# Four weight units of the first feed-forward panel have their low parts subtracted on GpSimd

## The chip, the cores and the metric

The kernel runs on one core of one Trainium2 chip. The metric is the device time of one execution in microseconds (us). Before the change it is 1159.51 us, the median of 3 runs (1159.35 to 1160.35).

Names: PE is TensorE, DVE is VectorE, ACT is ScalarE, POOL is GpSimd, SP is SyncE, which issues the loads.

## The reference

One decoder layer on 256 tokens of width 2048, all in float32. What matters here is the middle: an output projection with a residual, an RMS norm, and the feed-forward part of width 5632.

```python
h = h + jnp.concatenate([o_attn, o_conv], axis=-1) @ w_out[i]
f = rmsnorm(h, g_ffn[i])
h = h + (jax.nn.silu(f @ w_gate[i]) * (f @ w_up[i])) @ w_down[i]
```

## The kernel before, in words

**Every matrix product is done in parts.** A float32 operand is split into a high part (`hi`, rounded to the matmul's input type by a copy) and a low part (`lo`, the raw value minus `hi`). A product is then three matmuls: hi by hi, hi by lo and lo by hi. The weights stream from memory, so each piece of weights is split on the chip before its matmuls.

**The weights move in units.** Unit m is 128 partitions by 1024 numbers, half of a raw slot of 1 MB. Three steps handle it: ACT writes `w_hi` (line 666), then DVE or POOL writes `w_lo` (`split_lo`, line 993 on DVE and line 590 on POOL), then PE runs the unit's 12 matmuls. The units are numbered through the program. Unit 80 begins the output projection (`WO_A`), units 112 to 127 (`FFN0` to `LOOP0` - 1) are the first panel of 512 columns of the feed-forward part, and from 128 (`LOOP0`) on come ten passes of the main loop, the last panel and the gates.

**Slots.** `w_hi` and `w_lo` have four slots each, unit m uses slot m % 4. So ACT may write unit m + 4 only when PE has finished unit m (`slot_free`), and it does so about three units ahead of PE's need.

**Who subtracts.** `by_pool(m)` decides. Before the change POOL takes every fourth unit from 8 on and every second one from 40 up to 95; from unit 96 on DVE subtracts all. PE waits for the unit on the semaphore of the engine that subtracts it (`arrived`), and SP waits for both before it loads new weights over the raw slot (`slot_split`).

**The order is written out by hand.** Each engine has its own program, and its instructions run strictly one after the other. DVE and ACT go through steps m; step m ends with the split of unit m + 4. Around the change DVE's steps hold more than splits, because the main loop's products need the normed activations in another form:

- line 1277 in step 117: a row of scales is copied to `rb`
- line 1223 (`normalise`), two in each of the steps 118 to 121, tiles of 128x512 in `w_sum`
- lines 1238 to 1243 (`x_sums`), four sums of 128x256, in steps 119 and 120
- line 1229 (`a_lo`) in steps 119 to 123 and 125, and line 1249 (`s_lo`) in steps 120 and 121: low parts of what these gave; ACT makes their high parts (lines 873 and 878), the one of line 878 just ahead of units 124 and 125
- step 127: `first_swiglu` (line 1209), which waits for PE to finish the first panel; the main loop's first steps come right behind it on DVE.

All of these except line 1277 and line 1209 are two-input operations with both inputs in SBUF.

**POOL's program** after unit 95: eight additions that join the high and low parts of the activations (`join_x`, line 596), with a tiny `pow` (line 584) between the sixth and the seventh, then another tiny `pow` (`root(2, 3)`) that waits until the gates near the end of the kernel. Between 359.6 and 1072 us POOL does nothing.

Of the kernel before, what the change touches and what calls it, by code (L numbers as in the profile page):

```python
# [67 lines left out]
FFN0 = WO_C + 16  # L68
LOOP0 = FFN0 + 16
# [30 lines left out]
OUT_VECTOR = [(0, slice(0, 2 * NP)), (1, slice(0, NP)), (1, slice(NP, 2 * NP))]  # L100
OUT_SCALAR = [(0, slice(2 * NP, 3 * NP)), (1, slice(2 * NP, 11 * NP // 4)), (1, slice(11 * NP // 4, 7 * D // 8))]
POOL_HALF, POOL_UNTIL = 40, WO_C

# [27 lines left out]


def by_pool(m):
    return 8 <= m < POOL_UNTIL and (m % 4 == 3 or m % 2 == 1 and m >= POOL_HALF)


def lo_count(m, it=0):

    return sum(by_pool(i) == by_pool(m) for i in range(m + 1)) + PER_LOOP * it
# [32 lines left out]
def hybrid_decoder_layer(nc, x, p, g_mix, w_in, w_dw, b_dw, g_conv_ln, b_conv_ln, w_out, g_ffn,  # L174
# [11 lines left out]
    with ExitStack() as ctx:  # L186
# [85 lines left out]
        def x_norm(i):  # L272

            return w_sum[:, i].rearrange("p (k t) -> p k t", k=2)
# [93 lines left out]
        def slot_free(engine, m, it=0):  # L368

            if LAST <= m < LAST + 4:  # L370
                engine.wait_ge(half_done, PG0)
            elif m >= LAST + 4:
                engine.wait_ge(half_done, m - 2 * SLOTS + 1)
            elif LOOP0 + SLOTS <= m < LOOP0 + LOOP_SLOTS:

                engine.wait_ge(half_done, FFN0)
            elif in_loop(m) and m >= LOOP0 + LOOP_SLOTS:
                engine.wait_ge(half_done, m - slot_back(m) + 1 + PER_LOOP * it)
            elif PLE0 <= m < PLE0 + SLOTS:
                engine.wait_ge(half_done, m - PER_LOOP % LOOP_SLOTS + 1)  # L380
            elif m >= SLOTS:
                engine.wait_ge(half_done, m - SLOTS + 1)
# [49 lines left out]
        def _(sp):  # L432
            def slot_split(n, it=0):

                if n >= RAW:
                    last = 2 * (n - RAW) + 1
                    if by_pool(last):
                        sp.wait_ge(lo_ready, lo_count(last - 1))
                        sp.wait_ge(lo_ready_pool, lo_count(last))
                    else:  # L440
                        sp.wait_ge(lo_ready, lo_count(last, it))
# [125 lines left out]
        def _(pool):  # L567
# [11 lines left out]
            def root(norm, order, tiles=slice(0, TT)):  # L579

                if order == 0:
                    pool.wait_ge(consts_ready, 2)
                pool.wait_ge(msq_ready, order + 1)
                nc.gpsimd.tensor_tensor(rstd[:, norm, tiles], msq[:, norm, tiles], power[:, tiles], ALU.pow).then_inc(rstd_ready, 1)  # L584

            def split_lo(m):
                pool.wait_ge(hi_ready, m + 1)
                slot_free(pool, m)
                rows = slice(2 * (m % 2), 2 * (m % 2) + 2)
                nc.gpsimd.tensor_tensor(w_lo[:, m % SLOTS], w_raw[:, (m // 2) % RAW, rows],  # L590
                                        w_hi[:, m % SLOTS].bitcast(F32), ALU.subtract).then_inc(lo_ready_pool, 1)

            def join_x(i):

                pool.wait_ge(nT_ready, 4 + i // 2 + 1)
                nc.gpsimd.tensor_tensor(x_norm(i), nT_hi[:, 2 * i:2 * i + 2].bitcast(F32), nT_lo[:, 2 * i:2 * i + 2].bitcast(F32),
                                        ALU.add).then_inc(x_joined, 1)

            for m in filter(by_pool, range(POOL_UNTIL)):
                if m == AHEAD + 15:  # L600
                    root(0, 0)
                if m == AHEAD + 51:

                    pool.wait_ge(conv_step, CONV_OPS)
                    nc.gpsimd.tensor_tensor(group_sum[:, :, :], conv[:, 0:2], conv[:, 2:4], ALU.add).then_inc(conv_added, 1)
                    pool.wait_ge(conv_added, 1)
                    nc.gpsimd.tensor_tensor(group_sum[:, 0], group_sum[:, 0], group_sum[:, 1], ALU.add).then_inc(conv_added, 1)
                if m == AHEAD + MEAN_AT - 2:

                    pool.wait_ge(conv_step, 2 * CONV_OPS)  # L610
                    nc.gpsimd.tensor_tensor(u[:, 4:6, 0:T], conv[:, 4:6], conv[:, 6:8], ALU.add).then_inc(conv_added, 1)
                    pool.wait_ge(conv_added, 3)
                    nc.gpsimd.tensor_tensor(group_sum[:, 1], u[:, 4, 0:T], u[:, 5, 0:T], ALU.add).then_inc(conv_added, 1)
                if m == AHEAD + MEAN_AT + 2:
                    root(4, 1)
                if m == AHEAD + MEAN_AT:

                    for i in range(2):
                        pool.wait_ge(dev_squared, 2 * i + 2)
                        nc.gpsimd.tensor_tensor(u[:, 4 * i:4 * i + 2, 0:T], u[:, 4 * i:4 * i + 2, 0:T],  # L620
                                                u[:, 4 * i + 2:4 * i + 4, 0:T], ALU.add).then_inc(dev_added, 1)
                    pool.wait_ge(dev_added, 2)
                    nc.gpsimd.tensor_tensor(u[:, 0:2, 0:T], u[:, 0:2, 0:T], u[:, 4:6, 0:T], ALU.add).then_inc(dev_added, 1)
                split_lo(m)
# [2 lines left out]
            root(1, 2)  # L627
            for i in range(6, QUADS):
                join_x(i)
            root(2, 3)  # L630
            pool.wait_ge(rows_loaded, 32)
            for c in range(3):
# [1252 lines left out]
```

## Time and profile before

| | |
|---|---|
| median of 3 runs | 1159.51 us |
| the profiled execution | 1159.4 us |
| its span, first to last instruction | 1157.6 us |
| PE busy | 1142.3 us |
| DVE busy | 936.4 us |
| ACT busy | 717.0 us |
| POOL busy | 125.1 us |
| granted TensorE clock, mean | 0.998 |

The span is what the profile shows; 1.8 us of the profiled time lie around it. A busy PE means that matmuls follow each other without a gap, so each gap on PE is time that the kernel could be shorter, unless something else then comes in its place. The rows below have the first panel's units 121 to 127 between 369 and 389 us.

### The profile page before, as it was taken

To read this page: it belongs to the slowest core of one execution; us is meant where nothing else is said; L and a number is where in the kernel's file an instruction comes from. 1 tells how busy PE (TensorE), PEld (TensorE's weight loads), DVE (VectorE), ACT (ScalarE), POOL (GpSimd) and SP (SyncE) were. 2 spreads that over 40 slices of the span, in tenths; PEclk is the share of its full clock that TensorE was granted. 3 is DMA by queue.
4 is the path that set the end of the run, shared out by engine and by line. 5 is a ranking of instruction groups with operands and counts; after the bars stand their busy time and mean duration, and the time that the engine had idled before them with its cause. 6 is when DMAs were issued, how large, how long until landed. Compare 5 with 4: busy or idle time off the path is not lost.

```text
span 1157.6 us, 16551 instructions
## 1 busy us (share of the span) xinstructions
PE 1142.3 (99%) x5591; PEld 963.7 (83%) x5591; DVE 936.4 (81%) x1244; ACT 717.0 (62%) x990; POOL 125.1 (11%) x74
## 2 busy tenths in 40 slices
PE   9999999999999899999999999999999999999996
PEld 8889989988888678888888888888888888888886
DVE  6589767768677897989888898989798988847674
ACT  6544465456555576676767667676667676767552
POOL 0222443435031000000000000000000000000111
PEclk9999999999999999999999999999999999999999
DMA  9655554554555466575646564655647565484541
GB/s 343 217 182 182 182 181 158 172 170 158 189 175 181 146 227 209 170 241 171 234 165 226 176 247 149 227 180 193 232 160 242 178 228 172 153 317 152 202 158 73
DMA packets 113120, 223.38 MB, mean 193 GB/s; under 512 B 5193, under 2 KB 6417, under 8 KB 112816
## 3 DMA queue, kind: packets, MB, share of 16 engines
q1 hardware_dynamic: 112608, 222.08, 56.8%
q8 instruction: 29, 0.48, 0.2%
q10 hardware_dynamic: 464, 0.66, 0.2%
q14 instruction: 19, 0.16, 0.0%
HBM read 220.63 MB, written 2.10 MB: 192 GB/s over the span
## 4 chain that ended last, share of the span: by engine, by line
PE 91%; DVE 4%; issue 2%; ACT 1%; POOL 1%; DVEq 0%; POOLq 0%; ACTq 0%
PE ps L1679 11%; PE ps L1681 11%; PE ps L1680 11%; PE ps L1478 8%; PE ps L1476 8%; PE ps L1477 8%; PE ps L1463 6%; PE ps L1464 6%; PE ps L1465 6%; PE ps L1510 3%; PE ps L1509 3%; PE ps L1508 3%; PE ps L1518 2%; DVE w_lo L993 1%; PE ps L1672 1%
## 5 line engine op out<-in xcount | busy, mean ns | idle before, releaser
L666 ACT ACTIVATE w_hi<-w_raw 128x1024 fp32r<-128x1024 f32 (+1 forms) x308 | 304.2, 996 | 205.2 <-PE ps L1478 120.2
L993 DVE TENSOR_TENSOR w_lo<-w_raw,w_hi 128x1024 fp32r<-128x1024 f32 (+1 forms) x272 | 317.0, 1175 | 135.4 <-ACT w_hi L666 135.1
L1476 PE MATMUL ps<-w_hi,nT_hi 128*128 128x512 f32 x280 | 111.4, 398 | 0.0
L1478 PE MATMUL ps<-w_hi,nT_lo 128*128 128x512 f32 x280 | 109.1, 390 | 0.0
L1477 PE MATMUL ps<-w_lo,nT_hi 128*128 128x512 f32 x280 | 109.0, 389 | 0.0
L666 ACT ACTIVATE w_hi<-arena 128x1024 fp32r<-128x1024 f32 x58 | 61.6, 1062 | 73.9 <-DVE arena L1268 28.1
L590 POOL TENSOR_TENSOR w_lo<-w_raw,w_hi 128x1024 fp32r<-128x1024 f32 x36 | 86.7, 2408 | 181.9 <-ACT w_hi L666 181.9
L1049 DVE SCALAR_TENSOR_TENSOR ps<-arena,taps,ps 128x256 f32<-128x256 f32 x232 | 94.7, 485 | 0.2 <-ACT ps L787 0.2
L584 POOL TENSOR_TENSOR rstd<-msq,power 128x2 f32<-128x2 f32 x4 | 2.8, 707 | 724.4 <-DVE msq L1024 723.2
L993 DVE TENSOR_TENSOR w_extra<-w_raw,w_extra 128x1024 fp32r<-128x1024 f32 (+1 forms) x70 | 78.7, 1136 | 0.0
L1679 PE MATMUL ps<-w_hi,nT_hi 128*128 128x512 f32 x195 | 76.8, 394 | 0.0
L1681 PE MATMUL ps<-w_hi,nT_lo 128*128 128x512 f32 x195 | 76.0, 390 | 0.0
L1680 PE MATMUL ps<-w_lo,nT_hi 128*128 128x512 f32 x195 | 75.9, 389 | 0.0
L1508 PE MATMUL ps<-nT_hi,w_hi 128*128 128x256 f32 x256 | 72.9, 285 | 0.0
L1510 PE MATMUL ps<-nT_hi,w_lo 128*128 128x256 f32 x256 | 72.4, 283 | 0.0
L1509 PE MATMUL ps<-nT_lo,w_hi 128*128 128x256 f32 x256 | 72.4, 283 | 0.0
L993 DVE TENSOR_TENSOR w_lo<-arena,w_hi 128x1024 fp32r<-128x1024 f32 x58 | 69.1, 1220 | 0.0
L666 ACT ACTIVATE w_extra<-w_raw 128x1024 fp32r<-128x1024 f32 (+1 forms) x70 | 67.6, 980 | 0.5 <-PE ps L1681 0.2
L1476 PE MATMUL ps<-w_hi,oT_hi 128*128 128x512 f32 x160 | 63.5, 397 | 0.0
L853 ACT ACTIVATE ps<-h 128x512 f32<-128x512 f32 x80 | 44.9, 594 | 28.3 <-DVE arena L1271 26.7
L1478 PE MATMUL ps<-w_hi,oT_lo 128*128 128x512 f32 x160 | 62.4, 390 | 0.0
L1477 PE MATMUL ps<-w_lo,oT_hi 128*128 128x512 f32 x160 | 62.3, 389 | 0.0
(271 smaller groups left out, 2809.3 us busy)
## 6 DMA issues: line engine op xcount, KB each, us to landing
w_raw<-in_w_gate SPq DMA_DIRECT2D x88, 512.0 KB, 3.9
w_raw<-in_w_up SPq DMA_DIRECT2D x88, 512.0 KB, 4.8
w_raw<-in_w_down SPq DMA_DIRECT2D x44, 1024.0 KB, 5.1
w_raw<-in_w_in SPq DMA_DIRECT2D x32, 1024.0 KB, 5.1
w_raw<-in_w_out SPq DMA_DIRECT2D x16, 1024.0 KB, 5.0
w_raw<-in_w_pgate SPq DMA_DIRECT2D x16, 1024.0 KB, 5.1
w_raw<-in_w_in SPq DMA_DIRECT2D x14, 512.0 KB, 9.5
w_raw<-in_w_ple SPq DMA_DIRECT2D x2, 1024.0 KB, 5.8
```

The lines of the kernel that those rows point to most:

```text
L666: nc.scalar.activation(tiles_of(m, first)[0], source_of(m, first), ACT.Copy).then_inc(hi_ready, 1)
L993: nc.vector.tensor_tensor(lo, source_of(m, first), hi.bitcast(F32), ALU.subtract).then_inc(lo_ready, 1)
L1049: ins = nc.vector.scalar_tensor_tensor(dst, u[:, c, tap:tap + T], taps[:, c, tap:tap + 1], conv_sum(c), ALU.mult, ALU.add)
L1476: nc.tensor.matmul(banks[t][:, :], x_hi[:, k, rows], hi[:, k], start=start, stop=False)
L1477: nc.tensor.matmul(banks[t][:, :], x_hi[:, k, rows], lo[:, k], start=False, stop=False)
L1478: ins = nc.tensor.matmul(banks[t][:, :], x_lo[:, k, rows], hi[:, k], start=False, stop=stop)
L1508: nc.tensor.matmul(dst, w_hi[:, s, k, cols], x_hi[:, k], start=start, stop=False, skip_group_check=True)
L1509: nc.tensor.matmul(dst, w_hi[:, s, k, cols], x_lo[:, k], start=False, stop=False, skip_group_check=True)
L1510: ins = nc.tensor.matmul(dst, w_lo[:, s, k, cols], x_hi[:, k], start=False, stop=stop, skip_group_check=True)
L1679: nc.tensor.matmul(bank[:, :], x[0], w[0], start=first, stop=False)
L1680: nc.tensor.matmul(bank[:, :], x[0], w[1], start=False, stop=False)
L1681: return nc.tensor.matmul(bank[:, :], x[1], w[0], start=False, stop=last)
```

## The change

POOL takes the low parts of units 121, 123, 125 and 127. `by_pool` names them, so `arrived`, `slot_split` and the counts of both semaphores follow, DVE's program leaves them out, and POOL's program gets four calls of its `split_lo` between the last `join_x` and `root(2, 3)`.

```diff
 POOL_HALF, POOL_UNTIL = 40, WO_C
+POOL_FFN = range(FFN0 + 9, LOOP0, 2)
...
 def by_pool(m):
-    return 8 <= m < POOL_UNTIL and (m % 4 == 3 or m % 2 == 1 and m >= POOL_HALF)
+    return m in POOL_FFN or 8 <= m < POOL_UNTIL and (m % 4 == 3 or m % 2 == 1 and m >= POOL_HALF)
...
             for i in range(6, QUADS):
                 join_x(i)
+            for m in POOL_FFN:
+                split_lo(m)
             root(2, 3)
```

The three added lines move the lines behind them by one to three: line 993 is 996 in the changed kernel, line 590 is 591, line 1223 is 1226, 1229 is 1232, 1249 is 1252.

DVE's program before, from the end of step 120 on. The first and the last `w_lo` here are the splits of units 124 and 128; the rows with `arena,rb` are `normalise`, those with `nT_lo` are `a_lo`, and the one with `oT_lo` is `s_lo`:

```order
236 L993 TENSOR_TENSOR w_lo<-w_raw,w_hi 128x1024
237 L1223 TENSOR_TENSOR arena<-arena,rb 128x512 x2
238 L1229 TENSOR_TENSOR nT_lo<-arena,nT_hi 128x512
239 L1249 TENSOR_TENSOR oT_lo<-arena,oT_hi 128x1024
240 L993 TENSOR_TENSOR w_lo<-w_raw,w_hi 128x1024
241 L1229 TENSOR_TENSOR nT_lo<-arena,nT_hi 128x512
242 L993 TENSOR_TENSOR w_lo<-w_raw,w_hi 128x1024
243 L1229 TENSOR_TENSOR nT_lo<-arena,nT_hi 128x512
244 L993 TENSOR_TENSOR w_lo<-w_raw,w_hi 128x1024 x2
```

The same place in the changed kernel:

```order
234 L996 TENSOR_TENSOR w_lo<-w_raw,w_hi 128x1024
235 L1226 TENSOR_TENSOR arena<-arena,rb 128x512 x2
236 L1232 TENSOR_TENSOR nT_lo<-arena,nT_hi 128x512
237 L1252 TENSOR_TENSOR oT_lo<-arena,oT_hi 128x1024
238 L1232 TENSOR_TENSOR nT_lo<-arena,nT_hi 128x512
239 L996 TENSOR_TENSOR w_lo<-w_raw,w_hi 128x1024
240 L1232 TENSOR_TENSOR nT_lo<-arena,nT_hi 128x512
241 L996 TENSOR_TENSOR w_lo<-w_raw,w_hi 128x1024
```

The splits of unit 125 (row 240 of before) and of unit 127 (the first of the two in row 244) are gone from DVE; the splits of 124, 126 and 128 stand where they stood.

POOL's program in the changed kernel, from its last split before the feed-forward part on. The last `x4` row of `w_lo` is new; before, the row of `rstd` behind it followed the two additions directly:

```order
27 L591 TENSOR_TENSOR w_lo<-w_raw,w_hi 128x1024 x3
28 L597 TENSOR_TENSOR arena<-nT_hi,nT_lo 128x512 x6
29 L585 TENSOR_TENSOR rstd<-msq,power 128x2
30 L597 TENSOR_TENSOR arena<-nT_hi,nT_lo 128x512 x2
31 L591 TENSOR_TENSOR w_lo<-w_raw,w_hi 128x1024 x4
32 L585 TENSOR_TENSOR rstd<-msq,power 128x2
```

Only these four instructions were added to POOL's queue, and what stands behind them there is not due until the gates.

## Rows read from the trace of the kernel before

**Rows 1.** The page: the span, and each engine's busy time, share and instructions.
```profile
span 1157.6 us, 16551 instructions
PE 1142.3 (99%) x5591; PEld 963.7 (83%) x5591; DVE 936.4 (81%) x1244; ACT 717.0 (62%) x990; POOL 125.1 (11%) x74
```

**Rows 2.** Windows: stretch, length, busy us (instructions) of PE, PEld, DVE, ACT, POOL; clock, DMA, GB/s.
```profile
400.00:410.00 10.00, 7.25 (x30) 5.22 (x30) 9.96 (x12) 6.83 (x9) 0.00 (x0) 1.00 0.64 204
...
1150.00:1157.00 7.00, 0.00 (x0) 0.00 (x0) 2.29 (x7) 1.12 (x2) 0.55 (x1) 0.66 0.42 150
```

**Rows 3.** Timeline of PE, 379 to 406 us: start, duration, operation, [idle before, releaser].
```profile
379.65 0.39 PE L1673 MATMUL ps<-w_lo,nT_hi 128*128 128x512 f32 x1
379.88 0.39 PE L1674 MATMUL ps<-w_hi,nT_lo 128*128 128x512 f32 x1
380.57 0.50 PE L1672 MATMUL ps<-w_hi,nT_hi 128*128 128x512 f32 x1 [0.31 <-DVE w_lo L993]
...
405.78 0.50 PE L1679 MATMUL ps<-w_hi,oT_hi 128*128 128x512 f32 x1 [2.35 <-DVE w_lo L993]
```

**Rows 4.** Timeline of DVE, 362 to 390 us.
```profile
362.41 1.23 DVE L993 TENSOR_TENSOR w_lo<-w_raw,w_hi 128x1024 fp32r<-128x1024 f32 x1 [1.45 <-ACT w_hi L666]
363.56 1.29 DVE L1223 TENSOR_TENSOR arena<-arena,rb 128x512 f32<-128x512 f32 x2
...
367.82 0.42 DVE L1239 TENSOR_TENSOR arena<-arena 128x256 f32<-128x256 f32 x1
...
369.55 1.22 DVE L993 TENSOR_TENSOR w_lo<-w_raw,w_hi 128x1024 fp32r<-128x1024 f32 x1
370.69 1.28 DVE L1223 TENSOR_TENSOR arena<-arena,rb 128x512 f32<-128x512 f32 x2
...
375.22 1.22 DVE L993 TENSOR_TENSOR w_lo<-w_raw,w_hi 128x1024 fp32r<-128x1024 f32 x1
376.35 1.29 DVE L1223 TENSOR_TENSOR arena<-arena,rb 128x512 f32<-128x512 f32 x2
...
379.30 1.22 DVE L993 TENSOR_TENSOR w_lo<-w_raw,w_hi 128x1024 fp32r<-128x1024 f32 x1
...
381.03 1.22 DVE L993 TENSOR_TENSOR w_lo<-w_raw,w_hi 128x1024 fp32r<-128x1024 f32 x1
...
385.64 1.23 DVE L993 TENSOR_TENSOR w_lo<-w_raw,w_hi 128x1024 fp32r<-128x1024 f32 x1
387.50 1.23 DVE L993 TENSOR_TENSOR w_lo<-w_raw,w_hi 128x1024 fp32r<-128x1024 f32 x1 [0.63 <-ACT w_hi L666]
389.95 1.41 DVE L1209 SCALAR_TENSOR_TENSOR arena<-ps,rstd,arena 128x512 f32<-128x512 f32 x2 [1.22 <-ACT arena L840]
```

**Rows 5.** Timeline of ACT, 366 to 379 us: high parts of units 123, 125 and 127.
```profile
366.76 1.06 ACT L666 ACTIVATE w_hi<-w_raw 128x1024 fp32r<-128x1024 f32 x1 [1.14 <-PE ps L1674]
...
374.56 1.05 ACT L666 ACTIVATE w_hi<-w_raw 128x1024 fp32r<-128x1024 f32 x1
...
377.64 1.06 ACT L666 ACTIVATE w_hi<-w_raw 128x1024 fp32r<-128x1024 f32 x1
```

**Rows 6.** Timeline of POOL, 32 to 278 us, three of its operations.
```profile
32.19 2.70 POOL L590 TENSOR_TENSOR w_lo<-w_raw,w_hi 128x1024 fp32r<-128x1024 f32 x1 [29.98 <-ACT w_hi L666]
...
273.10 2.37 POOL L590 TENSOR_TENSOR w_lo<-w_raw,w_hi 128x1024 fp32r<-128x1024 f32 x1
...
277.39 2.39 POOL L590 TENSOR_TENSOR w_lo<-w_raw,w_hi 128x1024 fp32r<-128x1024 f32 x1
```

**Rows 7.** Timeline of DVE beside them.
```profile
32.08 0.56 DVE L1074 TENSOR_TENSOR log_count<-log_count,multiple 128x384 f32<-128x384 f32 x1
...
273.13 3.43 DVE L993 TENSOR_TENSOR w_lo<-w_raw,w_hi 128x1024 fp32r<-128x1024 f32 x1
...
278.29 2.58 DVE L993 TENSOR_TENSOR w_lo<-w_raw,w_hi 128x1024 fp32r<-128x1024 f32 x1 [0.47 <-ACT w_hi L666]
```

**Rows 8.** POOL's line 590, all of it: duration ns min/median/max, first and last start.
```profile
L590 POOL TENSOR_TENSOR w_lo<-w_raw,w_hi x36: 2373/2402/2698, 32.2 to 288.0; 128x1024 fp32r<-128x1024 f32 x36
```

## The prediction, made before the changed kernel ran

> **What bounds the kernel now.** I read the page first: PE is busy for 1142.3 of 1157.6 us [rows 1], so only its gaps can be won, 15.3 us in all. Then PE's waits in order of time. Between the fill at the start and the end of the kernel they stand in one place, the end of the first feed-forward panel and the 35 us behind it, and all of them are for low parts from DVE: the first at 380.57 us, the largest at 405.78 us [rows 3]. The window of 400 to 410 us shows why: PE 7.25 us busy, DVE 9.96 us, POOL 0 [rows 2]. So DVE bounds this stretch, POOL is free, and the change takes work from the one and gives it to the other. Last I read DVE's timeline there [rows 4] and looked for places where DVE and POOL worked side by side [rows 6, 7], since that is what the change brings.
>
> Which row is which unit: the split that starts at 362.41 us is unit 121's, at 369.55 unit 123's, at 375.22 unit 124's, at 379.30 unit 125's, at 381.03 unit 126's, at 385.64 unit 129's, at 387.50 unit 130's [rows 4]. The high parts of 123, 125 and 127 start at 366.76, 374.56 and 377.64 us [rows 5]. PE starts unit 125 at 380.57 [rows 3]. One matmul follows another after 0.227 us (379.65 to 379.88 [rows 3], and eleven more like it), so a unit of 12 takes 2.72 us: unit 124 starts at 377.4, unit 126 at 380.57 + 2.72 + 0.12 = 383.4 us. The 0.12 is the longer first matmul after a gap (0.50 against 0.39 us [rows 3]).
>
> **What can be won.** Of the gaps only the first lies in front of `first_swiglu`. It costs 380.57 - 379.88 - 0.23 = 0.46 us. The later ones come at the end of a DVE chain that starts when PE has finished the panel: DVE sat idle for 0.63 us at 387.50 and 1.22 us at 389.95 us [rows 4], so it had caught up by then, and work taken from it earlier doesn't start that chain sooner than PE does. So the largest gain is 0.46 us, 0.04%. The 4.6 us that DVE no longer spends on four splits (1.14 us each, 369.55 to 370.69 [rows 4]) are not a gain by themselves. Unit 121's falls into idle time at once: DVE was idle for 1.45 us before it [rows 4], and its next split, of 122, waits for ACT as before.
>
> **What a split on POOL costs.** It takes 2.40 us (median of 36 [rows 8]) against 1.14. POOL has time: its program has nothing else that is due before the gates, and a unit's high part is ready two units ahead of PE. The question is what it does to DVE. Three places show it. At 273.10 both start a split; POOL's ends at 275.47, DVE's takes 3.43 us and ends at 276.56, which is 1.09 us after POOL's end. At 277.39 POOL's ends at 279.78 and DVE's at 280.87, again 1.09 us later [rows 6, 7]. So DVE did its whole 1.1 us of work behind POOL's. The other way round, POOL's split at 32.19 took 2.70 us in place of 2.40 beside a DVE addition that had begun 0.11 us before. So two operations that each read two tiles of SBUF don't overlap on the two engines: one holds and the other stands still. I take 2.35 us for one hold (start to start less the overlap of two records). Everything that DVE runs between 366 and 387 us is of that kind, and it runs nearly without idle time. There a split moved to POOL saves DVE 1.14 us and stops it for 2.35.
>
> The Trainium skill says the same in *SBUF — State Buffer*, "Who interferes with whom": a VectorE instruction with two SBUF inputs contends with a GpSimd instruction that reads SBUF, and whoever issues first keeps the others out for the whole instruction. It speaks against this change, and by "whoever issues first" a waiting GpSimd gets the next turn even while VectorE has work lined up; no row here shows such a case, and the sum for it follows from rows.
>
> **Step by step, POOL getting its turn at the next end of a DVE operation.**
>
> - Unit 121: POOL from 362.4 to 364.8, DVE has nothing that is due in it but ends the two `normalise` at 362.2. Nothing gained or lost.
> - Unit 123: high part ready at 366.76 + 1.06 = 367.82 [rows 5]. DVE is then in `x_sums` (367.82 [rows 4]); POOL takes over at about 368.2 and DVE resumes at 370.55, 2.4 late. It then skips the split of 123 (1.14): `normalise` of step 120 starts at 371.9 in place of 370.69. DVE is 1.2 us behind. PE needs 123 at 374.7: in time.
> - Unit 124, on DVE: 375.22 + 1.2 = 376.4 to 377.6. PE wants it at 377.4: a first gap of 0.2 to 0.3 us.
> - Unit 125: its high part stands behind that of `s_hi` on ACT, which waits for the second `x_sums`, so it ends at 375.61 + 1.2 = 376.8. POOL starts when DVE's split of 124 ends, 377.55, and ends at 379.9. PE needs it at about 380.5: the old gap of 0.46 is gone, the new one of 0.25 is there.
> - Unit 127: high part ready at about 379 (377.64 + 1.06, and a little later behind unit 123's slot). POOL asks at once after 125 and gets another 2.35 us, either directly or after one DVE operation of 0.6 us. Both lie ahead of unit 126's split on DVE.
> - Unit 126, on DVE: `normalise` of step 121 is late by 1.2 + 2.35 + 2.35 = 5.9 us; the split of 125 in between is gone, so 126 starts at 381.03 + 5.9 - 1.14 = 385.8 and ends at 387.0 us. PE has finished unit 125 at 383.4 and waits 3.7 us. It starts 126 at 387.1 in place of 383.4: **+3.7 us**.
> - Behind it: the split of 127 is gone from DVE too, which leaves it 5.9 - 2.3 = 3.6 us late, the same as PE; 128 to 130 are in time again. Unit 127's end and `first_swiglu` move by 3.7 us, and the chain behind them, with the gaps up to 422 us, moves as a whole. ACT and SP: the raw slot of units 126 and 127 is freed some 3 us later, no more than PE is late, and its next weights are unit 138's, ten units on, so the load hides.
>
> Sum: 3.7 us on the profiled 1159.4 gives 1163.1, and with the median 0.1 above the profiled execution **1163.2 us**, 0.3% slower. In short: three holds (7.05) less two splits (2.3) less the 1.15 us by which DVE was early for unit 126, and 0.1 for the restart.
>
> **Rivals.**
>
> - *POOL must wait until DVE's queue runs dry.* DVE's operations begin before the last has quite ended (1.14 us apart at 1.22 us each), and POOL may never get in between. It gets in for 123 at a small dependence gap of `x_sums`, but for 125 there is none from 377.5 to the end of `a_lo(5)`, which is the start of 129's split: 385.64 - 376.35 = 9.3 us of run [rows 4] less two splits gives 377.5 + 7.0 = 384.5. POOL ends at 386.9, and PE starts unit 125 there in place of 380.57: +6.3, **1165.8 us**. For it: nothing in the trace excludes it, since every shared stretch before has DVE idle behind one operation. Against it: in [rows 6, 7] POOL got in 0.3 us after it asked. With an idle stretch of 6.7 us on PE the clock could fall as well: it fell to half after PE's last matmul, in a stretch that shows a mean of 0.66, while 2.35 us of idle left it at 1.00 [rows 2]. Each 12-matmul unit at half clock would add 2.7 us, so up to 1168.5.
> - *The holds don't hurt here.* If DVE's operations of 0.3 to 0.7 us slipped in between, or if the stretches of [rows 7] had another cause, POOL's splits would be free: DVE would be 1.14 to 3.4 us ahead, the gap at 380.57 goes, and the time is 1159.5 - 0.46 = **1159.0 us**, not slower. It decides as long as all holds together cost DVE less than the two splits it saves before unit 126, 2.3 us, plus its 1.15 us of lead. For it speaks that POOL has 2 units of time for each split; against it the two equal 1.09 us.
> - *Part of it*: one of the three holds falls into a time when DVE waits for ACT, or 127's comes after unit 126. Then 7.05 becomes 4.7: +1.3 us, 1160.8, and unless 127 is then itself late, it stays there.
>
> **Numbers.** POOL in turn 55%, POOL starved 25%, part of it 8%, no cost 12%. The likeliest gives 1163.2. The range of 8 in 10 leaves out no cost and the part of the starved case in which the clock falls: 1160.8 to 1167.0 us. What a measurement of this kernel can tell from no change is about 0.2%, 2.3 us. The first two cases are slower by more; part of it and no cost lie within 0.2%, but for a little of the former and of the turn's own spread to either side; a gain over 0.2% would need more than DVE's gaps before 389 us hold: 1%. So faster 0.01, same 0.18, slower 0.81.
>
> **What would show it.** In the changed kernel's profile: four POOL splits between 362 and 390 us; DVE's `x_sums` or `normalise` operations of over 2 us beside them, ended at POOL's end plus their own length; a PE gap of 3 to 4 us before unit 126, waiting for DVE (right), or of 6 us before unit 125, waiting for POOL (starved); gaps at 399 to 422 us of the same length as before, only later. Wrong, if DVE's operations keep 0.69 and 1.22 us while POOL runs, if PE has no gap over 1 us before `first_swiglu`, or if the gaps behind it shrink.

## The result, and the profile after

The changed kernel takes 1165.26 us, the median of 6 runs (1163.44 to 1165.50), against 1159.51 before. Over all runs that are compared the ratio is 1.0042, with an interval of 1.0032 to 1.0052. That is 4.9 us slower, between 3.7 and 6.0. (The two medians are 5.7 us apart, since four of the six executions of the kernel before that ran beside it took 1159.35 to 1159.51 us, which by the later ones is its rarer, quicker kind; see unit 123 below.)

The profiled execution took 1165.5 us. Of the 6.1 us that were added to the span of [rows 1], 3.3 are PE's busy time, although it runs the same 5591 matmuls: some of them were slower. The other 2.8 are gaps.

```profile
span 1163.7 us, 16555 instructions
PE 1145.6 (98%) x5591; PEld 966.3 (83%) x5591; DVE 939.1 (81%) x1240; ACT 717.6 (62%) x990; POOL 135.9 (12%) x78
```

DVE's busy time went up by 2.7 us although four splits left it. The reason stands in POOL's timeline and in DVE's beside it, 362 to 395 us (start, duration, operation; line 1226 is `normalise`, 1244 is in `x_sums`):

```profile
362.47 2.40 POOL L591 TENSOR_TENSOR w_lo<-w_raw,w_hi 128x1024 fp32r<-128x1024 f32 x1 [2.92 <-ACT w_hi L669]
367.91 2.59 POOL L591 TENSOR_TENSOR w_lo<-w_raw,w_hi 128x1024 fp32r<-128x1024 f32 x1 [3.04 <-ACT w_hi L669]
376.76 5.82 POOL L591 TENSOR_TENSOR w_lo<-w_raw,w_hi 128x1024 fp32r<-128x1024 f32 x2 [6.26 <-ACT w_hi L669]
```

```profile
365.14 1.23 DVE L996 TENSOR_TENSOR w_lo<-w_raw,w_hi 128x1024 fp32r<-128x1024 f32 x1 [2.78 <-ACT w_hi L669]
...
368.16 2.62 DVE L1244 TENSOR_TENSOR arena<-arena 128x256 f32<-128x256 f32 x1
...
371.76 1.29 DVE L1226 TENSOR_TENSOR arena<-arena,rb 128x512 f32<-128x512 f32 x2
...
376.29 1.22 DVE L996 TENSOR_TENSOR w_lo<-w_raw,w_hi 128x1024 fp32r<-128x1024 f32 x1
377.42 5.71 DVE L1226 TENSOR_TENSOR arena<-arena,rb 128x512 f32<-128x512 f32 x2
...
385.39 1.21 DVE L996 TENSOR_TENSOR w_lo<-w_raw,w_hi 128x1024 fp32r<-128x1024 f32 x1
...
394.91 1.41 DVE L1212 SCALAR_TENSOR_TENSOR arena<-ps,rstd,arena 128x512 f32<-128x512 f32 x2 [1.50 <-ACT arena L843]
```

An operation of 0.42 us took 2.62, and the two `normalise` of step 121 took 5.71 in place of 1.29 [rows 4]. Asked for one by one in that stretch:

```profile
L1226 DVE TENSOR_TENSOR arena<-arena,rb x2: 2892/2892/2893, 377.4 to 380.2; 128x512 f32<-128x512 f32 x2
```

Each was held for 2.21 us (2.89 less 0.68). POOL's two splits and DVE's two operations took turns one by one. The split of unit 126 begins at 385.39; before, it was 381.03 [rows 4].

PE's timeline (the gap stands in brackets). Unit 124 starts at 377.65, 0.25 us after the 377.4 of the kernel before. The first long gap is the one before unit 126; the one at 380.57 [rows 3] is gone, and the last answers to 405.78 of [rows 3]:

```profile
377.65 0.47 PE L1675 MATMUL ps<-w_hi,nT_hi 128*128 128x512 f32 x1
...
382.95 0.39 PE L1677 MATMUL ps<-w_hi,nT_lo 128*128 128x512 f32 x1
386.66 0.50 PE L1675 MATMUL ps<-w_hi,nT_hi 128*128 128x512 f32 x1 [3.32 <-DVE w_lo L996]
...
388.66 0.63 PE L1676 MATMUL ps<-w_lo,nT_hi 128*128 128x512 f32 x1
...
410.74 0.50 PE L1682 MATMUL ps<-w_hi,oT_hi 128*128 128x512 f32 x1 [2.38 <-DVE w_lo L996]
```

And windows of the same kernel (columns as in [rows 2]; the clock is the third number from the right). From 388 to 391 us, right behind the first gap, and from 412 to 415, behind the last, the granted clock is 0.51 and 0.50, which is 1.2 of the 2.4 GHz, and matmuls come 0.43 us apart in place of 0.23:

```profile
388.00:391.00 3.00, 3.00 (x9) 2.32 (x8) 2.08 (x3) 0.00 (x0) 0.00 (x0) 0.51 0.89 332
...
412.00:415.00 3.00, 3.00 (x8) 2.35 (x9) 3.00 (x3) 2.54 (x4) 0.00 (x0) 0.50 0.92 320
```

The tally of the two profiled executions: PE starts unit 126 3.2 us later (386.66 against the 383.4 worked out above). `first_swiglu` is 4.96 us later (394.91 - 389.95), so another 1.7 us was lost in units 126 and 127, at half clock. The span is 6.1 us longer, so the last 1.1 us came behind it, where the second stretch at half clock lies. That last part is not the change's, as the runs below show.

### The profile page after: what moved, and what is told of

Its sections match the earlier page's. It is cut to its first block, busy times and chain, and to the rows that moved or that the text cites. A ratio compares the mean times of both kernels' runs of the same rounds, so it can differ in the third digit from the quotient of the medians.

```text
span 1163.7 us, 16555 instructions
## 1 busy us (share of the span) xinstructions
PE 1145.6 (98%) x5591; PEld 966.3 (83%) x5591; DVE 939.1 (81%) x1240; ACT 717.6 (62%) x990; POOL 135.9 (12%) x78
## 4 chain that ended last, share of the span: by engine, by line
PE 92%; DVE 4%; issue 2%; ACT 1%; POOL 1%; POOLq 0%; DVEq 0%; ACTq 0%
PE ps L1682 11%; PE ps L1683 11%; PE ps L1684 11%; PE ps L1481 8%; PE ps L1479 8%; PE ps L1480 8%; PE ps L1468 6%; PE ps L1467 6%; PE ps L1466 6%; PE ps L1513 3%; PE ps L1511 3%; PE ps L1512 3%; PE ps L1521 2%; PE ps L1675 1%; PE ps L1677 1%
## 5 line engine op out<-in xcount | busy, mean ns | idle before, releaser
L996 DVE TENSOR_TENSOR w_lo<-w_raw,w_hi 128x1024 fp32r<-128x1024 f32 (+1 forms) x268 | 312.2, 1173 | 138.5 <-ACT w_hi L669 137.9
L591 POOL TENSOR_TENSOR w_lo<-w_raw,w_hi 128x1024 fp32r<-128x1024 f32 x40 | 97.5, 2439 | 194.2 <-ACT w_hi L669 194.2
```

The lines of the kernel that those rows point to most:

```text
L996: nc.vector.tensor_tensor(lo, source_of(m, first), hi.bitcast(F32), ALU.subtract).then_inc(lo_ready, 1)
```

## The experiments

Each is compared with runs of the kernel before on the same chip; ratios have their 95% intervals.

**Single units.** The set `POOL_FFN` of the changed kernel is cut down:

```diff
-POOL_FFN = range(FFN0 + 9, LOOP0, 2)
+POOL_FFN = (FFN0 + 9,)                # only_121
+POOL_FFN = (FFN0 + 11,)               # only_123
+POOL_FFN = (FFN0 + 13, FFN0 + 15)     # only_125_127
```

Unit 121:

> POOL takes the split of unit 121 alone. Theory of the holds: POOL runs it at 362.5 to 364.8 us, where DVE has nothing that reads two tiles, so no operation of DVE is stretched, DVE's idle time before the split of 122 grows by 1.1 us, and the time is that of the kernel before: 1159.5 us, within 0.3. Rival (a split on POOL costs wherever it stands, by its 2.4 us or by the extra semaphore): slower by about a quarter of the change's 5.7 us, 1160.9.

Measured: ratio 0.9999 (0.9990 to 1.0008), 1160.26 us beside 1160.17. Its POOL and DVE timelines:

```profile
362.16 2.40 POOL L591 TENSOR_TENSOR w_lo<-w_raw,w_hi 128x1024 fp32r<-128x1024 f32 x1 [2.91 <-ACT w_hi L669]
```

```profile
364.83 1.23 DVE L996 TENSOR_TENSOR w_lo<-w_raw,w_hi 128x1024 fp32r<-128x1024 f32 x1 [2.77 <-ACT w_hi L669]
```

POOL's split ends as DVE, which had been idle for 2.77 us, begins. Nothing is stretched, and the interval leaves no room for the 1.4 us of the rival, so a split on POOL as such costs nothing that this run can see.

Unit 123:

> POOL takes the split of unit 123 alone. Holds: one operation of DVE near 368 us takes about 2.6 us, DVE is 1.2 us late from there, PE's gap before unit 125 grows from 0.5 to 1.7 us and the one before 126 stays away: +1.2 us, 1160.7. Rival (the loss comes only from POOL being late for 125 and 127): no change, 1159.5.

Measured: ratio 1.0006 (0.9997 to 1.0015), 1160.81 beside 1160.17. DVE and PE:

```profile
368.16 2.62 DVE L1244 TENSOR_TENSOR arena<-arena 128x256 f32<-128x256 f32 x1
```

```profile
381.63 0.50 PE L1675 MATMUL ps<-w_hi,nT_hi 128*128 128x512 f32 x1 [0.98 <-DVE w_lo L996]
```

The hold and the later start of unit 125 (381.63 against 380.57 [rows 3], +1.06) are as expected. The median rose by 0.6 us and its interval holds both 0 and the forecast 1.2. The record says why. The executions of a kernel fall into two groups by the mean of the granted clock that each reports. For the kernel before, in all the rounds of these experiments, 17 of 70 executions have 0.998 and took 1159.26 to 1159.71 us, the other 53 have 0.995 to 0.997 and took 1159.93 to 1160.94. Of this kernel 6 of 10 are in the group at 0.998, with 1160.46 to 1160.83, and 4 in the other, with 1161.02 to 1161.65. Group against group the medians differ by 1.1 and 1.2 us, which is the forecast. (The groups were formed after the runs, so this supports the size and is no test of it.)

Units 125 and 127:

> POOL takes 125 and 127 alone. Holds: both fall between the split of 124 and that of 126 on DVE, two operations of DVE take 2.9 us, the split of 126 ends near 385.9 and PE starts 126 2.5 us later than before; with the clock falling after such a gap another 1.5 to 3 us: 1162.0 without the fall, 1163.5 to 1165 with it. Rival (the three holds are not additive, one of them does the harm): the full 1165.

Measured: ratio 1.0023 (1.0014 to 1.0033); the median of 1162.46 beside 1160.17 hides a spread of 1161.84 to 1164.91. DVE and PE:

```profile
376.43 5.73 DVE L1226 TENSOR_TENSOR arena<-arena,rb 128x512 f32<-128x512 f32 x2
```

```profile
385.68 0.50 PE L1675 MATMUL ps<-w_hi,nT_hi 128*128 128x512 f32 x1 [2.62 <-DVE w_lo L996]
```

Two holds, and unit 126 starts 2.3 us later than before (385.68 against 383.4), near the forecast 2.5. The rival's full 1165 is not the median. The profiled execution took 1164.56 us and has the clock at 0.85 from 380 to 390; six of the ten took 1161.84 to 1162.47. So at least the 2.3 us of the wait seem to be in every execution, while the price of the clock comes and goes. Only the one execution was profiled.

**The saving without POOL.** DVE's four splits are shrunk to 8 of each 512 columns. The rest of these low parts is left out.

```diff
+                src = source_of(m, first)
+                if m in range(FFN0 + 9, LOOP0, 2):
+                    hi, lo, src = hi[:, :, 0:8], lo[:, :, 0:8], src[:, :, 0:8]
-                nc.vector.tensor_tensor(lo, source_of(m, first), ...)
+                nc.vector.tensor_tensor(lo, src, ...)
```

> Nothing on POOL; DVE's splits of units 121, 123, 125 and 127 cover only the first 8 of each 512 columns (the other low parts are left out, and PE multiplies what the slot held before). This is the change with its saving and without its cost. By the reading that DVE's lead can't be used behind the first panel: the gap at 380.57 goes and nothing else, -0.46 us, 1159.0. Rival (DVE's 4.2 us are worth more, since it bounds the stretch behind): up to -4 us, 1155.5.

Measured: ratio 0.9995 (0.9986 to 1.0004), 1159.53 beside 1160.17. The gap at 380.6 is gone, and the first gap left is the one that stood at 399.18 in the kernel before, with about the same size (1.10 there); `first_swiglu` starts at 389.47 against 389.95 [rows 4]:

```profile
398.71 0.50 PE L1682 MATMUL ps<-w_extra,nT_hi 128*128 128x512 f32 x1 [1.07 <-DVE w_extra L996]
```

So by the trace 4.2 us less work on DVE ahead of `first_swiglu` are worth 0.5 us. The interval goes from -1.6 to +0.5 us: the rival of -4 us is out, no gain at all is not. By the groups of executions there is a gain: three at 0.998 took 1158.40 to 1158.60, below all 70 of the kernel before.

**Four POOL operations that nobody needs, added to the kernel before.** DVE keeps all its splits. Once they read SBUF, once they only write it:

```diff
             for i in range(6, QUADS):
                 join_x(i)
+            for i, m in enumerate(range(FFN0 + 9, LOOP0, 2)):
+                pool.wait_ge(hi_ready, m + 1)
+                if i:
+                    pool.wait_ge(extra_done, i)
+                # extra_reads:
+                nc.gpsimd.tensor_tensor(arena[:, 0:1024], h[:, 0, 0:1024], h[:, 1, 0:1024], ALU.subtract).then_inc(extra_done, 1)
+                # extra_memset, in its place:
+                nc.gpsimd.memset(arena[:, 0:2600], 0.0).then_inc(extra_done, 1)
             root(2, 3)
...
                 split_hi(m + AHEAD)
+            sc.wait_ge(extra_done, 4)
```

`extra_done` keeps the four in order, since they write the same place, and ACT goes on behind the panel only when all are done. In neither profile does ACT show a wait for it.

> The kernel before, with four subtractions added on POOL that nobody needs, each of 128x1024 numbers from two pieces of h in SBUF, released at the same moments as the change's splits (high parts of 121, 123, 125 and 127 ready). DVE keeps all its splits. Holds: each stops DVE for 2.35 us and gives nothing back; DVE is about 9 us late at unit 126's split, PE 7.5 to 8 us, with the clock's falls on top 1168 to 1171 us. Rival (the change's loss comes from PE waiting for POOL's results, or from the semaphores): no change, 1160.

Measured: ratio 1.0096 (1.0080 to 1.0111), 1171.07 beside 1160.08. POOL, DVE and PE:

```profile
379.72 5.79 POOL L635 TENSOR_TENSOR arena<-h 128x1024 f32<-128x1024 f32 x2 [8.66 <-ACT w_hi L672]
```

```profile
380.40 5.66 DVE L1230 TENSOR_TENSOR arena<-arena,rb 128x512 f32<-128x512 f32 x2
```

```profile
380.63 0.47 PE L1679 MATMUL ps<-w_hi,nT_hi 128*128 128x512 f32 x1 [2.72 <-DVE w_lo L1000]
...
388.98 0.80 PE L1679 MATMUL ps<-w_hi,nT_hi 128*128 128x512 f32 x1 [3.77 <-DVE w_lo L1000]
```

These are units 124 and 125, which start 3.2 and 8.4 us later than in the kernel before. DVE's split of unit 126 begins 8.4 us later (389.45 against 381.03), near the 9 forecast. `first_swiglu` starts 9.7 us later (399.67), with the clock's falls in it, and the 11 us of the time are at the upper end of what was expected.

> The same, but the four added POOL instructions are memsets of 2600 numbers per partition, about 2.4 us each by the rate of the memsets at the kernel's start, which read no SBUF. Holds by two readers: no operation of DVE is stretched, 1160 us as before. Rival (any long POOL instruction that touches SBUF stops DVE): as in the run with the subtractions, 1168 or more.

Measured: ratio 0.9998 (0.9989 to 1.0008), 1160.17 beside 1160.08. POOL, DVE and PE:

```profile
375.67 2.28 POOL L635 MEMSET arena<- 128x2600 f32 x1 [5.51 <-ACT w_hi L672]
```

```profile
376.36 1.29 DVE L1230 TENSOR_TENSOR arena<-arena,rb 128x512 f32<-128x512 f32 x2
```

```profile
380.57 0.50 PE L1679 MATMUL ps<-w_hi,nT_hi 128*128 128x512 f32 x1 [0.31 <-DVE w_lo L1000]
```

This is the cleanest pair. No engine waits for either POOL operation in this stretch. Nearly as long as the subtractions (2.28 us against 2.40), the memsets leave the same two DVE operations at 1.29 us where the subtractions make them 5.66. So the loss is neither PE waiting for POOL's results nor POOL being busy, but two engines that each read SBUF operands: the one waits while the other works. A POOL operation that reads one tile only was not run. The Trainium skill states this distinction in *SBUF — State Buffer*, "Who interferes with whom" (a GpSimd instruction that only writes SBUF doesn't contend with a VectorE instruction of two SBUF inputs). These two traces agree.

**The clock.** Needless matmuls are put on PE ahead of unit 126 in the changed kernel, 28 and then 14:

```diff
+                if m == FFN0 + 14:
+                    for _ in range(28):      # fill_126; 14 in fill_14
+                        nc.tensor.matmul(ps[4][:, 0:P], mean_w[:, :], mean_w[:, :], start=True, stop=True)
                 gate_and_up(m)
```

> The changed kernel, with 28 matmuls of 128x128 that nobody needs put into PE's gap before unit 126, into a bank that is free there (28 x 0.11 = 3.1 us, the gap is 3.7). If the fall of the clock from 388 to 391 us is PE's reaction to the gap, the clock stays full there and the first panel ends 1.6 us sooner: 1163.6 against the changed kernel's 1165.3. Rival (the fall comes from something else, the load of the chip or its timing): 1165.3, with the fall at the same place.

Measured: ratio 1.0054 (1.0038 to 1.0069), 1166.57 beside 1160.08, no faster than the change. I had mis-sized the filler:

```profile
383.53 6.41 PE L1788 MATMUL ps<-mean_w 128*128 128x128 f32 x56
```

A float32 matmul is recorded as two here, and 28 took 6.2 us. PE was late by itself, so this run says nothing on the time, only that the clock stayed at 1.00 from 380 to 400 us. The second try:

> The changed kernel with 14 such float32 matmuls before unit 126 in place of 28. In the run with 28 each took two passes, 0.22 us in all, so they lasted 6.2 us and not 3.1; 14 should last 3.1 and fit into the gap of 3.7. If the clock's fall is PE's answer to the gap: the panel's end comes 1.5 us sooner than in the changed kernel, 1163.7. Rival: 1165.3.

Measured: ratio 1.0026 (1.0016 to 1.0036), 1163.44 beside 1160.21. PE's timeline, then windows:

```profile
382.66 3.29 PE L1788 MATMUL ps<-mean_w 128*128 128x128 f32 x28
386.10 0.50 PE L1675 MATMUL ps<-w_hi,nT_hi 128*128 128x512 f32 x1 [0.15 <-DVE w_lo L996]
```

```profile
380.00:390.00 10.00, 9.85 (x58) 8.52 (x57) 9.52 (x9) 3.41 (x4) 2.02 (x1) 1.00 0.59 190
390.00:400.00 10.00, 10.00 (x50) 8.37 (x49) 6.89 (x8) 3.51 (x6) 0.00 (x0) 1.00 0.39 126
```

This execution is 0.56 us ahead of the changed kernel's from the start of the stretch (POOL's split of unit 121 at 361.91 against 362.47), so unit 126 at 386.10 answers to 386.66 there: DVE is as late, PE comes to unit 126 as late, but it isn't idle, and the clock stays at 1.00. `first_swiglu` starts at 392.77 against 394.91, which is 1.6 us sooner beyond the 0.56, as expected. The time is 1.8 us below that of the change (0.0016 between the ratios; the intervals just overlap). So in these traces the clock falls where PE stood idle ahead of unit 126 and stays up where it had matmuls to run, and the fall is worth about what the trace says (1.7 us). What is left, +3.2 us (1163.44 - 1160.21), is the wait alone, and with the 1.7 it makes the 4.9 us of the change.

**Where DVE's time would be worth something.** These start from the kernel before and move nothing to POOL. `early_sums` takes the weight sums of the main loop's first seven-product quad (three operations, 2.4 us) in front of `first_swiglu`; `early_both` also has `normalise` one step earlier; `early_more` also shifts three operations behind it:

```diff
-NORMAL_AT = [RB1_AT + 1 + i // 2 for i in range(QUADS)]
+NORMAL_AT = [RB1_AT + i // 2 for i in range(QUADS)]      # early_both, early_more
...
                 if m == LOOP0 - 1:
+                    for half in range(2):
+                        weight_sums(half, 0, S_FIRST)
                     ve.wait_ge(panel_read, Q_DOWN)
                     first_swiglu()
...
                 if m == LOOP0 + SLOTS + 2:
+                    weight_sums(0, 0, S_QUADS[1])            # early_more
                     act_lo(ACT_BANKS, 0)
-                if m in (LOOP0 + SLOTS, LOOP0 + SLOTS + 1):
-                    weight_sums(m - LOOP0 - SLOTS, 0, S_FIRST)
                 split_lo(m)
-            weight_sums(0, 0, S_QUADS[1])                    # early_more, and
-            for i in (QUADS - 2, QUADS - 1):                 # these a_lo go to
-                a_lo(i)                                      # t == 6 of the first pass
```

> The kernel before with DVE's work reordered and nothing moved to POOL: the weight sums of the main loop's first seven-product quad (three operations, 2.4 us) run before first_swiglu, in the 0.6 and 1.2 us in which DVE is idle, and normalise stands one step earlier. If the lead that DVE has at the panel's end was only useless because nothing was left to do, this makes it useful: the gaps at 399.2 and 400.4 go, the one before 405.8 shrinks to 1 us or less, the one at 380.6 goes; -3 to -4 us, 1156.5. Rival (ACT, or first_swiglu's delay, takes the place of DVE): within 1 us of before.

> The kernel before with only the weight sums of the first seven-product quad ahead of first_swiglu, normalise where it was. If the gaps behind the panel are set by DVE's work between first_swiglu and the split of unit 135: they shrink by about 2.5 us, 1157.5; the gap at 380.6 (0.46) stays. Rival (the earlier normalise is what made the last version faster): 1160.

> The last version, with two more moves on DVE: the first weight sum of the second quad goes into the 1.0 us in which DVE waits for ACT before act_lo, and the two a_lo of quads 6 and 7 (1.2 us) go behind the split of unit 140. DVE's split of 135 is then ready about 2.2 us sooner, before PE asks for it at 400.1: the gap of 1.7 us and the stretch at half clock behind it go, -2.5 to -3 us against 1157.0, 1154.3. Rival (the gap only moves to about 415 us, where the two a_lo now stand): 1156 to 1157.

Measured:

| kernel | expected | us | before, beside it | ratio |
|---|---|---|---|---|
| `early_sums` | 1157.5 | 1158.03 | 1160.21 | 0.9979 (0.9970 to 0.9989) |
| `early_both` | 1156.5 | 1157.01 | 1160.08 | 0.9973 (0.9962 to 0.9984) |
| `early_more` | 1154.3 | 1155.40 | 1160.21 | 0.9959 (0.9946 to 0.9973) |

In `early_both` the gaps at 380, 399 and 400 us are gone and the one that was 2.35 is 1.74, with the clock at 0.83 in that window. Expected was 1 us or less. In `early_sums` it is 1.77, and only the gap at 380.57 is still there. So nearly all of the gain comes from the weight sums:

```profile
402.26 0.50 PE L1679 MATMUL ps<-w_hi,oT_hi 128*128 128x512 f32 x1 [1.74 <-DVE w_lo L993]
```

```profile
400.00:410.00 10.00, 8.11 (x28) 5.92 (x27) 9.93 (x12) 5.65 (x7) 0.00 (x0) 0.83 0.52 165
```

In `early_more` this window has PE busy 9.94 us (7.25 in [rows 2]) and the clock at 1.00; part of the gap came back at 415 to 418 us, 0.8 us in three pieces:

```profile
400.00:410.00 10.00, 9.94 (x44) 7.91 (x43) 9.96 (x12) 5.55 (x7) 0.00 (x0) 1.00 0.66 203
```

```profile
415.39 0.47 PE L1680 MATMUL ps<-w_hi,nT_hi 128*128 128x512 f32 x1 [0.42 <-DVE w_lo L993]
...
417.23 0.50 PE L1680 MATMUL ps<-w_hi,oT_hi 128*128 128x512 f32 x1 [0.21 <-DVE w_lo L993]
418.36 0.50 PE L1680 MATMUL ps<-w_more,oT_hi 128*128 128x512 f32 x1 [0.17 <-DVE w_more L993]
```

It beats both kernels: 4.8 us below the one before, and 9.9 below the changed one's 1165.26. I had expected 1154.3; the rival that the gap comes back behind it has a share. Between `early_sums` and `early_both` the intervals overlap, so they don't settle what `normalise` one step earlier is worth. In the groups by clock `early_both` is the quicker one in both: 1156.36 to 1156.55 against 1156.79 to 1157.23 at 0.998, and 1157.01 to 1157.44 against 1157.60 to 1158.12 in the rest.

## Why the prediction was right, point by point

- **DVE and POOL exclude each other where both read two tiles of SBUF.** Right, and shown: stretched operations in six kernels (the changed one, `only_123`, `only_125_127`, `extra_reads` and both with the filler), none beside memsets.
- **Who gets the turn.** The forecast was "POOL at the next end of a DVE operation", and it was so. For 125, POOL asked at 376.76 and DVE's split of 124 ended at about 377.4; the next `normalise`, already lined up, waited. Then they alternated one by one. This was a step of the prediction's own that no row of the kernel before showed. The starved case, 25%, is out: PE never waited for POOL. The time alone would not have said so, since that rival's 1165.8 lies nearer to the measured 1165.26 than the forecast 1163.2; it is the trace that decides between them.
- **The size of a hold.** Taken as 2.35 us, measured 2.20 (2.62 - 0.42, and 2.89 - 0.68 twice). Three holds make 6.6 and not 7.05, so PE waited until 386.66 and not 387.1: +3.2 in place of +3.7. This term was too large by 0.45 us. The rest of the chain came as forecast: the 0.25 us before unit 124, the end of the gap at 380.57, DVE's split of unit 126 at 385.39 (forecast 385.8).
- **Unit 121 is free, and DVE's lead is worth the 0.46 us of one gap.** The first is shown. The second holds in the trace of `short_splits`: no gap before the panel's end, the next one unchanged, `first_swiglu` 0.48 us sooner.
- **The gaps behind the panel move as a whole.** Right for their lengths: 2.38 at 410.74 against 2.35 at 405.78.
- **What the forecast had at nothing: the clock.** I let it fall only in the starved case, since 2.35 us of idle had left it at 1.00 in the one trace. In the changed kernel it fell behind 3.3 us of idle, +1.7 us, and this is most of what lies between the forecast 1163.2 and 1165.26. As a change, 4.9 us were measured and 3.7 forecast: the missing 1.7 less the 0.45 of the holds. That the second error made up for a part of the first is luck.
- **The second fall is no work of the change.** The clock also fell behind the gap of 2.4 us, at 412. In `only_121` and `extra_memset`, which take the time of the kernel before, it has the same dip behind that gap, 0.87 and 0.83 in these two rows:

```profile
400.00:410.00 10.00, 7.33 (x24) 5.31 (x25) 9.96 (x13) 6.55 (x9) 0.00 (x0) 0.87 0.61 207
```

```profile
400.00:410.00 10.00, 7.38 (x25) 5.46 (x25) 9.97 (x12) 6.87 (x9) 0.00 (x0) 0.83 0.61 203
```

Both of these profiled executions report a mean clock of 0.996. The profiled execution of the kernel before (1159.4 us) had no dip and 0.998, the value that only 17 of its 70 later executions have; the medians of the two kinds are 1159.4 and 1160.2 us. So the likeliest reading is that three in four executions of the kernel before have this fall, at about 0.8 us, and that the trace from which I forecast was of the rarer kind. This adds 0.8 us to the distance between the forecast 1163.2 and the measured 1165.26, and nothing to the change. No execution with the fall was profiled for that kernel.
- Of the rivals, "the holds don't hurt here" is refuted by the stretched operations and by `extra_reads`; "part of it" by the three holds in the trace.

## What to carry to other kernels

Before work goes from VectorE to GpSimd, look at what VectorE runs beside it: if those are operations with two SBUF inputs and no idle time between them, as here, a split moved away saves VectorE 1.1 us and holds it for 2.2 us in the same place, and only in VectorE's idle stretches was it free. Time saved on an engine counts from the next point where it waits for nobody; here the work behind `first_swiglu` had to be brought forward into the idle time. That alone gave 0.2%, and with the further moves of `early_more` 0.4%. A gap on TensorE can have a second price, the matmuls at half clock behind it, and one profiled execution doesn't tell how often it is paid; the mean clocks and times of all executions tell more.

## What was not expected

- The clock's fall comes after the gap, when PE has been back at work: restart at 386.66, matmuls 0.23 us apart until 388.2, then 0.43 apart until 391.2, granted clock 0.51. Whether it comes behind a gap of 2.4 us differs between executions: 1.00 in the kernel before from 406 us on, 0.50 in the changed one from 412 us on.
- Kernels with such gaps have the wider times. `only_125_127`, with gaps of 2.6 and 2.4 us, runs from 1161.84 to 1164.91; `early_more`, with none above 0.42 us in this stretch, from 1155.25 to 1155.58.
- Turns between the two engines are given one by one: 2.89 us for each of two DVE operations of 0.68 us, with a POOL operation before each.
